# A chain of six blocks on one core: weights in seven half-size slots, the last four weight tiles of a product taken token tile by token tile, modulation in units of two blocks by two column halves

## The reference

```python
def trunk_layer(x, cx, ...):              # twice
    sh1, sc1, ga1, sh2, sc2, ga2 = modulation(c, w_mod, b_mod)      # silu(c) @ w_mod + b_mod, 6 x 1024
    u = (rmsnorm(x, g_mix) * (1 + sc1) + sh1) @ w_in                # width 2080
    mix = concat([pool_mixer(p), gla_output(o_gl), latent_attention(ql, k_all, v_all)]) @ w_out
    x = x + ga1 * mix
    x = x + ga2 * squared_relu_mlp(rmsnorm(x, g_mlp) * (1 + sc2) + sh2, w_up, w_down)   # hidden 4096
def second_block(x, ...):
    x = x + gated_deltanet(rmsnorm(x)); x = x + swiglu(rmsnorm(x))  # hidden 2816
    x = x + dilated_attention(rmsnorm(x)); x = x + swiglu(rmsnorm(x))
```

## Time and profile before

| | us |
|---|---|
| Median of 3 runs | 2166.85 (2166.06 to 2183.19) |
| the profiled execution | 2179.32 |
| its span, first to last instruction | 2177.3 |
| TensorE busy | 1948.7 (90%) |
| VectorE busy | 1025.7 (47%) |
| ScalarE busy | 810.9 (37%) |
| GpSimd busy | 301.8 (14%) |
| mean granted TensorE clock | 0.911 |

### The profile page before, as it was taken

One profiled execution on the slowest core, in us unless ns is written; L12 is line 12 of the kernel. 1 busy time (PEld: TensorE's weight loads), 2 busy tenths in 40 slices (PEclk: granted clock), 3 DMA queues, 4 the chain that ended last, 5 costly groups with the idle time before them and its releaser, 6 DMA issues.

```text
span 2177.3 us, 27114 instructions
## 1 busy us (share of the span) xinstructions
PE 1948.7 (90%) x11407; PEld 1646.1 (76%) x11407; DVE 1025.7 (47%) x1519; ACT 810.9 (37%) x1298; POOL 301.8 (14%) x359
## 2 busy tenths in 40 slices
PE   5888789979999998868989977988899999988999
PEld 2676456768888887644788967977789977868997
DVE  2236552253333335255455545764355545575553
ACT  3422232243223234423344534433244434434443
POOL 1003100121212221020111210021200004300000
PEclk8898686789999999978899988999899999999999
DMA  7223332312332322253445543420055554503554
GB/s 267 78 97 141 111 117 78 135 58 78 97 97 97 97 80 87 66 196 107 144 135 194 174 146 97 136 78 20 23 167 175 182 186 157 197 23 116 183 185 135
DMA packets 182069, 268.83 MB, mean 123 GB/s; under 512 B 7606, under 2 KB 102522, under 8 KB 181692
## 3 DMA queue, kind: packets, MB, share of 16 engines
q1 hardware_dynamic: 176740, 257.32, 35.9%
q0 software_dynamic: 1744, 6.03, 0.8%
q10 hardware_dynamic: 3464, 3.75, 0.5%
HBM read 266.03 MB, written 1.05 MB: 123 GB/s over the span
## 4 chain that ended last, share of the span: by engine, by line
PE 77%; DVE 10%; ACT 5%; POOL 2%; DMA 2%; issue 2%; SPq 0%; POOLq 0%; DVEq 0%; ACTq 0%
PE ps L69 74%; PE ps L77 3%; DVE WLO L86 2%; DVE AR L96 2%; DVE AR L86 2%; DMA RAW<-in_w_mod_dram 1%; ACT WHI L80 1%; POOL SM L86 1%; ACT AR L80 1%; POOL XR L86 1%; DVE SM L99 1%; DMA RAW<-in_w_in_dram 1%; DVE TL L86 1%; ACT TH L80 1%; ACT XR L80 1%
## 5 line engine op out<-in xcount | busy, mean ns | idle before, releaser
L86 DVE TENSOR_TENSOR WLO<-RAW,WHI 128x1024 fp32r<-128x1024 f32 (+2 forms) x402 | 470.1, 1211 | 339.1 <-ACT WHI L80 339.0
L80 ACT ACTIVATE WHI<-RAW 128x1024 fp32r<-128x1024 f32 (+2 forms) x402 | 390.0, 1020 | 336.8 <-PE ps L69 319.6
L69 PE MATMUL ps<-TH,WHI 128*128 128x256 f32 (+1 forms) x1408 | 433.7, 308 | 21.1 <-DVE WLO L86 14.1
L69 PE MATMUL ps<-TL,WHI 128*128 128x256 f32 (+1 forms) x1408 | 431.8, 307 | 0.0
L69 PE MATMUL ps<-TH,WLO 128*128 128x256 f32 (+1 forms) x1408 | 431.4, 306 | 0.0
L69 PEld LDWEIGHTS ps<-TH,WHI 128*128 128x128 f32 x1408 | 275.5, 196 | 33.5 <-issue 19.6
L69 PEld LDWEIGHTS ps<-TL,WHI 128*128 128x128 f32 x1408 | 275.4, 196 | 10.1
L69 PEld LDWEIGHTS ps<-TH,WLO 128*128 128x128 f32 x1408 | 275.2, 195 | 10.2
L80 ACT ACTIVATE AR<-ps 128x512 f32<-128x512 f32 (+3 forms) x255 | 120.0, 488 | 420.0 <-PE ps L69 348.0
L69 PE MATMUL ps<-WHI,TH 128*128 128x512 f32 (+3 forms) x624 | 245.5, 393 | 11.7 <-DVE WLO L86 11.2
L69 PE MATMUL ps<-WLO,TH 128*128 128x512 f32 (+3 forms) x624 | 236.8, 379 | 0.0
(11 more groups left out here) (169 smaller groups left out, 2300.6 us busy)
## 6 DMA issues: line engine op xcount, KB each, us to landing
RAW<-in_w_mod_dram SPq DMA_DIRECT2D x48, 1024.0 KB, 6.7
RAW<-in_ffn_w_in_dram SPq DMA_DIRECT2D x44, 1024.0 KB, 5.1
RAW<-in_w_up_dram SPq DMA_DIRECT2D x32, 1024.0 KB, 5.4
RAW<-in_w_down_dram SPq DMA_DIRECT2D x32, 1024.0 KB, 5.1
RAW<-in_ffn_w_out_dram SPq DMA_DIRECT2D x20, 1024.0 KB, 5.0
RAW<-in_dil_w_in_dram SPq DMA_DIRECT2D x18, 1024.0 KB, 5.0
RAW<-in_gdn_w_in_dram SPq DMA_DIRECT2D x16, 1024.0 KB, 5.7
RAW<-in_w_in_dram SPq DMA_DIRECT2D x12, 1024.0 KB, 6.0
```

Source lines behind the costliest of these rows:

```text
L69: return Made(None if self.eng is None else self.eng.matmul(o, l, r, start=start, stop=stop))
L80: return Made(None if self.eng is None else self.eng.activation(o, i, f, **k))
L86: return Made(None if self.eng is None else self.eng.tensor_tensor(o, a, b, op))
```

## The change

- **Half-size tiles.** 2 x 512 or 4 x 256 columns (512 KB, 1024 elements in a partition). Seven slots (NS). WLO lies over RAW: the low part is written in place. So every load now waits for TensorE to have used the tile seven places earlier.
- **Splits.** `act_ahead` and `dve_ahead` split up to five tiles (AHEAD) beyond the step that their stream has come to, one instruction for a half tile. `projections_cap` is gone.
- **Order of a product.** `row_steps`: up to the last four half tiles, weight tiles outside and token tiles inside; the last four, token tile by token tile. A product with 8 row blocks has only these four. "used" is said at the last token tile.
- **Norms.** The norm of a finished token tile is done while later ones are computed, in both blocks, since `pe_out` now uses `pe_closed`.
- **Modulation.** A unit is four half tiles, each four matmuls of 32 x 256 (two row blocks by two column halves); ROWS is 256 wide, SEL has two columns for each half. Units 4 to 7 and 16 to 19 are placed beside gr, pq, kv and akv: one quarter after each of the last token tile's steps. LAG is 6, DLAG 7. The unit's copy is 2 steps, its turn 4 and DVE's part 5 steps behind.
- **Small things.** pm comes in two half tiles; lring has three banks in the projections and gring three; the shares of one weave in gdn are 23 in place of 24.

```diff
-NRAW = 3
-NW = 2
-LAG = 3
+NS = 7
+AHEAD = 5
+ROWK = 2
+LAG = 6
...
-        RAW = sb("RAW", NRAW * 2048)
-        whi0 = here()
-        WHI = sb("WHI", NW * 2048, F32R)
-        wlo0 = here()
-        WLO = sb("WLO", NW * 2048, F32R)
+        raw0 = here()
+        RAW = sb("RAW", NS * 1024)
+        WLO = alias("WLO", NS * 1024, F32R, raw0)
+        WHI = sb("WHI", NS * 1024, F32R)
...
         def load_weights():
             for t in tiles:
-                if t.i >= NRAW:
-                    had = tiles[t.i - NRAW]
-                    if had.j is None:
-                        sp.wait_ge(pe_gemm, ("used", had.i))
-                    else:
-                        sp.wait_ge(dve_w, ("lo", had.i, 1))
+                if t.i >= NS:
+                    sp.wait_ge(pe_gemm, ("used", t.i - NS))
                 src = T[t.name] if t.name == "pm" else T[t.name][t.idx]
                 src = src[128 * t.k0:128 * (t.k0 + t.nk), t.c0:t.c0 + t.n].rearrange("(k p) n -> p k n", p=128)
-                sp.dma(t.of(t.raw), src).then_inc(w_land[t.i % NRAW], t.i)
-
-        def halves_of(t):
-            n = t.nk * t.n
-            return ((0, 0, n // 2), (1, n // 2, n))
-
-        def act_splits(upto):
-
-            while act.j <= min(upto, act.cap, len(split_tiles) - 1):
-                t = split_tiles[act.j]
-                for h, a, b in halves_of(t):
-                    act.wait_ge(w_land[t.i % NRAW], t.i)
-                    if t.j >= NW:
-                        act.wait_ge(pe_gemm, ("used", split_tiles[t.j - NW].i))
-                    act.act(t.hi[:, a:b], t.raw[:, a:b], ACT.Copy).then_inc(act_w, ("hi", t.i, h))
+                sp.dma(t.of(t.raw), src).then_inc(w_land[t.i % NS], t.i)
+
+        def act_ahead(t):
+
+            while act.j < len(tiles) and act.j <= t.i + AHEAD:
+                w = tiles[act.j]
+                if w.split:
+                    act.wait_ge(w_land[w.i % NS], w.i)
+                    n = w.nk * w.n
+                    act.act(w.hi[:, 0:n], w.raw[:, 0:n], ACT.Copy).then_inc(act_w, ("hi", w.i))
                 act.j += 1
...
+        def row_steps(ws, tls):
+
+
+            n = len(ws)
+            head = max(0, n - 4)
+            return ([(c, ti, c) for c in range(head) for ti in tls] +
+                    [(c, ti, c if ti == tls[-1] else head) for ti in tls for c in range(head, n)])
         def pe_rows(key, ws, tls, lhs, need):
-            n, nk = ws[0][5], sum(w[3] for w in ws)
-            for c, w in enumerate(ws):
-                t = use(*w)
+            n, last_c, nk = ws[0][5], len(ws) - 1, sum(w[3] for w in ws)
+            for c, ti, _ in row_steps(ws, tls):
+                t = use(*ws[c])
                 hi, lo = t.of(t.hi), t.of(t.lo)
-                for ti in tls:
-                    if c == 0:
-                        banks.take((key, ti), gring)
-                        wait_free((key, ti))
-                    o = banks.of((key, ti))[:, 0:n]
-                    for k in range(t.nk):
-                        kk = t.k0 - ws[0][2] + k
-                        pe.wait_ge(dve_w, ("lo", t.i, 2 * k // t.nk))
-                        need(kk, ti)
-                        lh, ll = lhs(kk, ti)
-                        m = pe.matmul3(o, lh, ll, hi[:, k, :], lo[:, k, :], kk == 0, kk == nk - 1)
-                    said = [("used", t.i)] if ti == tls[-1] else []
-                    if c == len(ws) - 1:
-                        said.append(("acc", key, ti))
-                    if said:
-                        m.then_inc(pe_gemm, *said)
-                    yield
+                if c == 0:
+                    banks.take((key, ti), gring)
+                    wait_free((key, ti))
+                o = banks.of((key, ti))[:, 0:n]
+                pe.wait_ge(dve_w, ("lo", t.i))
+                for k in range(t.nk):
+                    kk = t.k0 - ws[0][2] + k
+                    need(kk, ti)
+                    lh, ll = lhs(kk, ti)
+                    m = pe.matmul3(o, lh, ll, hi[:, k, :], lo[:, k, :], kk == 0, kk == nk - 1)
+                said = [("used", t.i)] if ti == tls[-1] else []
+                if c == last_c:
+                    said.append(("acc", key, ti))
+                if said:
+                    m.then_inc(pe_gemm, *said)
+                yield ti if c == last_c else None
...
+        def pe_modulate(m, q):
             l, ch = chunks[m]
-            b = banks.take(("mod", m), ring)
-            wait_free(("mod", m))
-            for k0 in (0, 4):
-                t = use("w_mod", l, k0, 4, 512 * ch, 512, False)
-                v = t.of(t.raw)
-                pe.wait_ge(w_land[t.i % NRAW], t.i)
-                for k in range(4):
-                    i = pe.matmul(b[32 * k:32 * k + 32, :], SC2[:, k0 + k, :], v[:, k, :], k0 == 0, k0 == 4)
-                i.then_inc(pe_gemm, ("used", t.i), ("mod", m))
+            if q == 0:
+                banks.take(("mod", m), ring)
+                wait_free(("mod", m))
+            b = banks.of(("mod", m))
+            t = use("w_mod", l, 2 * q, 2, 512 * ch, 512, False)
+            v = t.of(t.raw)
+            pe.wait_ge(w_land[t.i % NS], t.i)
+            for g in range(4):
+                k, h = g // 2, g % 2
+                i = pe.matmul(b[32 * g:32 * g + 32, 0:256], SC2[:, 2 * q + k, :], v[:, k, 256 * h:256 * h + 256], q == 0, q == 3)
+            i.then_inc(pe_gemm, ("used", t.i), ("mod", m))
...
+                    if (m := beside(l, n)) is not None and ti == tls_of(n, l)[-1]:
+                        pe_modulate(m, c)
+                if (m := ended_name(l, s - 4)) is not None:
+                    pe_modturn(m)
                 if r := given(steps, s - LAG):
                     if (l, r[0], r[2]) in TURNED:
                         pe_feature(l, r[0], r[2])
                 yield
+
+
+        def beside(l, n):
+            i = NAMES.index(n)
+            return (4 if l == 0 else 16) + i if i < 4 else None
+
+        def ended_name(l, s):
+
+            r = given(PSTEPS[l], s)
+            return beside(l, r[0]) if r and r[2] == tls_of(r[0], l)[-1] else None
...
         def dve_closed(gkey, specs, tls, residual, t):
-            n = len(tls)
-            steps = n * len(specs)
-            for s, _ in enumerate(dve_rows(gkey, specs, tls)):
-                i = s - (steps - n)
-                if i >= 0:
-                    residual(tls[i])
-                    if t:
-                        dve_behind(t, tls, i)
+            done, since, m = 0, 0, min(4, len(specs))
+            modulated = t in ("mlp0", "in1", "mlp1")
+
+            def norm(i):
+                (dve_norm if modulated else dve_row)(t, tls[i], tls[i - 2] if i >= 2 else None)
+            for ti in dve_rows(gkey, specs, tls):
+                done, since = (done + 1, 0) if ti is not None else (done, since + 1)
+                if ti is not None:
+                    residual(ti)
+                if t and done >= 2 and since == min(2, m - 1):
+                    dve_turned(t, tls[done - 2], modulated)
+                if t and done and since == m - 1:
+                    norm(done - 1)
             if t:
-                for i in (n, n + 1):
-                    dve_behind(t, tls, i)
-
-        def dve_behind(t, tls, i):
-            n = len(tls)
-            if 1 <= i <= n:
-                dve_norm(t, tls[i - 1], tls[i - 3] if i >= 3 else None)
-            if 2 <= i:
-                dve_turned(t, tls[i - 2], True)
+                dve_turned(t, tls[-2], modulated)
+                norm(len(tls) - 1)
+                dve_turned(t, tls[-1], modulated)
...
-        MODS = [(range(4, 8), range(8, 16)), (range(16, 20), range(20, 24))]
+        MODS = [range(8, 16), range(20, 24)]
...
-        def projections_cap(engine, l):
-
-            engine.cap = tile_of["w_in", l, 4, COLS[NAMES[-1]][0]].j
-
         def mixers(l, project, attention, pooling, gla, mods):
-            p, gs, m = project(l), [gla(l, sq) for sq in range(2)], [mods(x) for x in MODS[l]]
+            p, gs = project(l), [gla(l, sq) for sq in range(2)]
             advance(p, solo(l))
             k = keyed(l)
             weave((part(p, k), k), *[(part(g, n), n) for g, n in zip(gs, EARLY[l])])
-            weave((p, left(l) - k), *[(part(g, n), n) for g, n in zip(gs, LATE[l])], (m[0], 2 * len(MODS[l][0])))
+            weave((p, left(l) - k), *[(part(g, n), n) for g, n in zip(gs, LATE[l])])
             yield
             rest = [(g, n - e - d) for g, n, e, d in zip(gs, FULL[l], EARLY[l], LATE[l]) if n > e + d]
-            weave((attention(l), souls(l)), (pooling(l), 1 + len(SEQS[l])), (m[1], 2 * len(MODS[l][1])), *rest)
+            weave((attention(l), souls(l)), (pooling(l), 1 + len(SEQS[l])), (mods(MODS[l]), 3 * len(MODS[l])), *rest)
...
-                gring.set(0, 1, 2, 3)
-                lring.set(4, 5)
+                gring.set(0, 1, 2)
+                lring.set(3, 4, 5)
                 ring.set(6, 7)
```

(1 more changed line is left out.)

312 lines of the change are left out of this document (149 added, 163 removed).

## The result

| | us |
|---|---|
| changed kernel, median of 4 runs | 2240.24 (2232.07 to 2244.41) |
| kernel before, median of 4 runs | 2175.02 (2166.06 to 2185.21) |
| ratio of the two | 1.0294, 95% interval 1.0227 to 1.0361 |
| span of the profiled execution after (before 2177.3) | 2240.6 |

The ratio is worked out from the single executions; it is not the quotient of the two medians, here and in the table of the experiments. The executions of the kernel before lie in two groups in every comparison, about 2159 to 2173 us and 2176 to 2189 us (mean granted clock 0.913 to 0.922 and 0.906 to 0.918), and the profiled one is of the upper, so a difference of under 20 us between two kernels can be a matter of which group an execution is in.

What follows compares the result with a forecast made beforehand. The kernel was taken as bound by TensorE's work plus its idle time, about 228 us. Costs of 45.5 less gains of 34.3 gave +11.2 on the median 2166.85, so 2178.1, stated as 2178.3; range 2143 to 2205.

Steps and rivals of the forecast that it cites:

- 6.1 us from slot to usable tile: Every half tile: landing 3.6, ACT's half 1.05, DVE's 1.25, hops about 0.2, from TensorE's release to use.
- (i): Norms: last residual and norm chain stand behind DVE's split of a late tile, until E+3.3 (E: product's end); 9.1 us cost.
- (a): Projections: w_in loads asked for earlier with seven slots, so the holes of 8.50 and 8.05 shrink; 14.5 us gained.
- (b): Projections: less low granted clock behind the two large holes and in the slow feature stretches; 6 us gained.
- The rival that w_in still comes late: Projections: eight-in-seven limit makes w_in wait for the same steps, so the gains at its holes are lost; 2198 us, chance 0.10.
- (e): A third bank for gate matmuls saves one round per layer, 2 us; modulation turns four steps behind save 3 us.
- (f): Projection product boundaries: eight half tiles over seven slots make TensorE wait 3.6, 2.7, 2.3 and 2.9 per layer; 23 us cost.
- (g): Projections: slow clock behind the four largest boundary waits, 1.6 us each; 6.4 us cost.
- (h): Before w_out, units 14 and 22: ACT and DVE held at its first half tile, attention work behind; 3.5 each, 7 us cost.
- Edits I cost at nothing: MLPs and FFNs keep 2 us or more of slack for half tiles, gdn conv stays ACT/DVE bound, smaller ROWS and SEL off the path; 0.
- the place of the 6.32: Start of gdn: TensorE's 6.32 us wait for ACT's queued w splits goes, with splits five half tiles ahead; 6.3 us gained.
- the slower rival: In-order hold pays in full, at all eight boundaries and w_out; decides if a boundary costs over 4.2; 2195 us, chance 0.25.

Runs made afterwards that it cites:

- e3: Changed kernel with modulation units 4 to 7 and 16 to 19 moved from beside the projections into attention, AHEAD still 5: 2187.1 us, ratio 1.0074 to the kernel before.
- e12: Changed kernel with modulation in attention, AHEAD 3, splits behind each step's work, and ACT's turn before the last tile's squares: 2155.4 us, ratio 0.9924 to the kernel before.
- e1: Changed kernel with AHEAD 3 in place of 5, nothing else: 2196.9 us, ratio 1.0095 to the kernel before.
- e5: Changed kernel with modulation units 4 to 7 and 16 to 19 in attention and AHEAD 3: 2164.8 us, ratio 0.9933 to the kernel before.
- e7: Kernel before (three slots, 1 MB tiles) with only modulation units 4 to 7 and 16 to 19 moved into attention: 2165.9 us, ratio 0.9953 to the unedited one.

## Why the prediction was wrong, by its steps

- **The number that all rests on, 6.1 us from slot to usable tile.** It was mis-sized. Its landing of 3.6 came from four loads; after, most loads share the way with one or two others and take 4.7 to 5.3. Step (i) put the residual at E+3.3 and it stood at E+4.7.
- **(a) and (b), 20.5 us back.** The waits of 8.50 and 8.05 vanished, but waits of 7.00+3.33 and 5.95 came at the same places. The rival that w_in still comes late, to which I gave 0.10, holds for aq in both layers. Of (e), the third bank gave what I said (the gate waits of 6.22 and 6.15 are 5.36 and 5.29); the waits ahead of the turns fell from 7.0 to 1.6 us over the whole trace, but in layer 0 TensorE now waits 5.3 us elsewhere for the copies of the units (1.08, 1.28 and 2.95).
- **(f) boundaries, 23 us.** Measured waits for DVE's split: 3.55, 2.67, 0.66, 7.00+3.33 in layer 0 and 3.94, 4.14, 0.45+1.02, 5.95 in layer 1: 32.7. The mechanism was right. That the first two came out at 3.55 and 2.67 against 3.6 and 2.7 is luck: from slot to usable tile took 7.2 and 7.7 us and not 6.1, and from the slot's return to the product's end 3.7 and 5.0 and not 2.5 and 3.6. One cause is that a quarter of a unit, which I put at 0.25 by counting four matmuls, shows eight in the trace and took 0.64. aq was mis-sized by two causes that I left out: in layer 0 the load took 7.0 us, and DVE came to it behind gate work.
- **(g) clock, 6.4.** The granted clock fell to half at six of the eight boundaries and not at four; it stayed at full behind the two short ones (0.66 and 0.45+1.02). Against e3 the products' matmuls are 5.8 and 7.4 us longer, 13 in both layers: twice the price.
- **(h) before w_out, 7 us.** 4.33 and 5.43 at units 14 and 22, above the price of 3.5 each; 7.68 at unit 15 was missing. Together 17.4.
- **(i) norms, 9.1.** Measured 20.8. Besides the landing, two things failed: ffn1, which I had at nothing, lost 3.5, and "the new code does the first norms under the product" bought nothing: the first norm, put at -1.4, lost 1.7. One cause is that the last token tile's norm waits in a queue behind the turn of the one before (e12, 3.9 us of the norms); the rest of it is open.
- **"Edits I cost at nothing".** The largest miss in us is in projections and attention (19.3, the steps above); this is the step that failed in kind, since it had no term at all: +12.3 in the dilated stage, +5.4 in the first MLP. I asked there whether TensorE gets its next half tile in time, and it does. I did not ask what else stands behind the split on ACT and DVE, though I did ask it for the norms. The same hold sits at every place where a stage's last step is followed by work on these engines.
- **Right:** gdn's weight matmuls no longer wait at the place of the 6.32; ffn0, the second MLP and ffn1 lost next to nothing (+0.1, +0.6 and +1.4); and the slower rival had the mechanism and its direction. That the whole gdn stage gave -6.0 against -6.3 proves little, since with the same code it took 8 us more in e3.

The slower rival said 2195 and "the in-order hold pays in full". Its mechanism was this one, at more places than the projections, and its time was 45 us too low; a boundary cost 4.1 us in the mean, just under the 4.2 that it asked for. Taking the hold away gives 43 us by e1, taking modulation away from the boundaries 53 by e3, both together 75 by e5.

The section of the Trainium skill that I weighed, "DMA: Bandwidth & Descriptors", "Anatomy of one DMA — SWDGE (gpsimd) path", gives a fixed part and bytes for one DMA. An estimate by it is 3.2 us for 512 KB. For a load alone the trace stayed near that form (3.5 and 3.6 us here). For half tiles under way with others it was off by 1 to 3 us, and that estimate would have made my sum still smaller.

## What to carry to other kernels

When a wait moves earlier in an in-order queue, list everything behind it at each stage end, not only at the place that the edit was made for; splitting further ahead is not free when the slot comes back late. Count slots against what is in flight at a boundary (here four and four against seven) before interleaving a second stream of loads; that the count alone is what costs was not tested. Try the small version first: moving the modulation out of the projections gave the kernel before 0.5% without any of the rest. With three tiles ahead the new scheme reaches 0.4 to 0.8%. The intervals of the two overlap (e7 0.9920 to 0.9986, e5 0.9899 to 0.9966, e12 0.9887 to 0.9962), so it isn't shown that half tiles, seven slots and the new order are worth anything beyond the small version; and all of it is below the 1% that the prediction took as the least that can be told from no change.

## What the runs showed of the hardware

- The landing of a load goes with its neighbours as much as with its size here. In the run after, 512 KB took 3.75 us in the median with no other weight load under way at its issue, 4.68 with one, 5.34 with two and 6.72 with three; 1 MB had 5.0 in the kernel before. I had expected a half tile to land in 3.6 anywhere.
- Halving the tiles and doubling the instructions for loads cost nothing that could be seen where TensorE is the limit: ffn0, with 66 half tiles, took 188.67 us against 188.54.
- Short waits of TensorE are followed by the low clock too. In the run after, the granted clock fell to half behind boundary waits of 3.55 and 2.67 us, and stayed there for 20 us around those of 7.00 and 3.33.
